# Dividing the last query block's two weight loads into 120 and 8 partitions

## What is computed

```python
q = jnp.einsum('bsd,dq->bsq', h, w_q).reshape(b, s, PEER_HEADS, 2, PEER_HALF)
s1 = jnp.einsum('bshq,hnq->bshn', q[..., 0, :], keys1)
s2 = jnp.einsum('bshq,hnq->bshn', q[..., 1, :], keys2)
v1, i1 = lax.top_k(s1, PEER_TOPK)
v2, i2 = lax.top_k(s2, PEER_TOPK)
...
best, pos = lax.top_k(cand, PEER_TOPK)
expert_idx = jnp.take_along_axis(cand_idx, pos, axis=-1)
gates = jax.nn.softmax(best.astype(jnp.float32), axis=-1).astype(h.dtype)
...
    u = jnp.take(u_tab, ix, axis=0)
    act = jax.nn.gelu(jnp.einsum('chkd,cd->chk', u, hx), approximate=False)
    vv = jnp.take(v_tab, ix, axis=0)
    return jnp.einsum('chk,chkd->cd', gx * act, vv)
```

## Time and profile before

| | us |
|---|---|
| median of 3 runs (1844.26 to 1846.62) | 1845.99 |
| the profiled execution, whole | 1844.33 |
| its span in the trace | 1841.7 |
| DMA from software queue, share of 16 engines | 79.4% |
| DMA from hardware queue, share of 16 engines | 16.5% |
| TensorE busy | 1475.1 |
| VectorE busy | 1142.5 |

### The profile page before, as it was taken

How to read it: one execution, slowest core, us unless ns; L and a number is a source line. 1 busy time by engine, 2 the same in 40 slices (tenths; PEclk the granted TensorE clock), 3 DMA queues, 4 the chain that set the end, 5 groups by cost and what they waited for, 6 DMA issues and landing times.

```text
span 1841.7 us, 13707 instructions
## 1 busy us (share of the span) xinstructions
PE 1475.1 (80%) x4834; PEld 828.1 (45%) x4834; DVE 1142.5 (62%) x1562; ACT 350.9 (19%) x697; POOL 620.3 (34%) x625
## 2 busy tenths in 40 slices
PE   2979998899899897777777777777877777777776
PEld 2549986777788633232323323233322323232332
DVE  5858886688789955555555555538555555544445
ACT  3004332663301211010011101101111111010100
POOL 0001111001154773444343443417643443433341
PEclk9889999999999899999999999998999999999999
DMA  9999998459879999999999999999999999999995
GB/s 341 386 389 404 399 354 326 176 187 379 323 303 413 421 421 421 422 422 422 422 421 422 422 422 422 422 421 402 422 422 422 422 422 421 422 422 422 422 422 233
DMA packets 138241, 716.43 MB, mean 389 GB/s; under 512 B 11158, under 2 KB 15436, under 8 KB 63692
## 3 DMA queue, kind: packets, MB, share of 16 engines
q0 software_dynamic: 82976, 604.02, 79.4%
q1 hardware_dynamic: 55212, 111.77, 16.5%
HBM read 713.65 MB, written 2.10 MB: 389 GB/s over the span
## 4 chain that ended last, share of the span: by engine, by line
DMA 58%; DVE 15%; PE 15%; POOL 6%; issue 4%; ACT 1%; SPq 1%; DVEq 0%; POOLq 0%; ACTq 0%
DMA u_rows<-in_peer_u,expert 49%; DVE u_rows L1740 6%; PE ps L768 4%; DMA v_rows<-in_peer_v,expert 4%; DVE first_acc L454 3%; POOL v_rows L665 3%; POOL u_rows L665 3%; PE ps L762 2%; DMA ada_first<-in_w_ada 2%; PE ps L425 2%; DMA ada_late<-in_w_ada 2%; PE ps L927 2%; DVE ada_acc L293 2%; DMA u_rows<-in_peer_v,expert 1%; PE ps L732 1%
## 5 line engine op out<-in xcount | busy, mean ns | idle before, releaser
L1012 PE MATMUL ps<-v_rows,diag 128*128 128x512 f32 x1960 | 905.6, 608 | 269.8 <-DMA v_rows<-in_peer_v,expert 255.6
L1740 DVE SCALAR_TENSOR_TENSOR u_rows<-u_rows,h 128x2048 f32<-128x2048 f32 x256 | 587.1, 2293 | 519.5 <-DMA u_rows<-in_peer_u,expert 514.7
L1012 PEld LDWEIGHTS ps<-v_rows,diag 128*128 128x128 f32 x1960 | 358.8, 191 | 815.2 <-issue 586.5
L665 POOL DMA_INDIRECT u_rows<-in_peer_u,expert x256 | 284.9, 1113 | 621.1 <-DVE u_rows L1740 576.4
L665 POOL DMA_INDIRECT v_rows<-in_peer_v,expert x249 | 287.2, 1153 | 97.0 <-issue 78.6
L1339 ACT ACTIVATE diag<-ident,hidden 128x128 f32<-128x128 f32 x250 | 89.6, 398 | 847.8 <-PE ps L1012 534.2
L293 DVE SCALAR_TENSOR_TENSOR ada_acc<-ada_late,cact,ada_acc 128x2048 f32<-128x2048 f32 x57 | 133.9, 2349 | 19.5 <-DMA ada_late<-in_w_ada 18.5
L279 POOL DMA_DIRECT2D ada_late<-in_w_ada x61 | 32.4, 532 | 321.9 <-DVE ada_acc L293 275.8
L981 PE MATMUL ps<-h2T,ring 128*128 128x256 f32 x512 | 117.7, 390 | 6.4 <-DMA ring<-in_w_peer_q 6.4
L981 PEld LDWEIGHTS ps<-h2T,ring 128*128 128x128 f32 x512 | 99.6, 197 | 20.6 <-DMA ring<-in_w_peer_q 6.8
L454 DVE SCALAR_TENSOR_TENSOR first_acc<-ada_first,cact,first_acc 128x1024 f32<-128x1024 f32 x60 | 77.0, 1284 | 16.9 <-DMA ada_first<-in_w_ada 11.5
(11 more groups left out here) (273 smaller groups left out, 1256.4 us busy)
## 6 DMA issues: line engine op xcount, KB each, us to landing
ada_late<-in_w_ada POOLq DMA_DIRECT2D x61, 1024.0 KB, 7.7
ada_first<-in_w_ada SPq DMA_DIRECT2D x64, 512.0 KB, 11.7
ring<-in_w_in SPq DMA_DIRECT2D x10, 2048.0 KB, 23.5
ring<-in_w_o SPq DMA_DIRECT2D x8, 2048.0 KB, 19.1
ring<-in_w_peer_q SPq DMA_DIRECT2D x8, 2048.0 KB, 14.3
opened<-in_w_in SPq DMA_DIRECT2D x8, 1024.0 KB, 13.0
u_rows<-in_peer_u,expert POOLq DMA_INDIRECT x256, 32.2
v_rows<-in_peer_v,expert POOLq DMA_INDIRECT x249, 34.2
```

The lines of the kernel that those rows point to most:

```text
L665: nc.gpsimd.indirect_dma_start(buf[:, :], None, table, bass.IndirectOffsetOnAxis(ap=expert[:, q, k:k + 1], axis=0)).then_inc(done, 16)
L1012: ins = nc.tensor.matmul(ps[:, c, :], diag[i % len(diag)][:, :], buf[:, 512 * c:512 * c + 512], start=(n % HALF_SLOTS == 0), stop=last)
L1740: nc.vector.scalar_tensor_tensor(out=buf[:, :], in0=buf[:, :], scalar=1.0, in1=h2[:, q // H, :], op0=ALU.mult, op1=ALU.mult, accum_out=hid ...
```

## The change

Each half of w_pq3 is loaded by two transfers, one of partitions 0 to 119 and one of partitions 120 to 127, issued one behind the other on SP, both on the semaphore of that half of the ring. The plan counts two transfers for each half of that block, so TensorE waits for both. w_pq0 to w_pq2 are loaded as before.

```diff
-    def load_half(eng, name, half, view, col, width=512):
+    def load_half(eng, name, half, view, col, width=512, rows=((0, P),)):
         chunks = slice(KH * half, KH * half + KH)
         w = ring[item[name][0]][:, :].rearrange("p (kc n) -> p kc n", kc=KC)
-        load(eng, name, half, (w[:, chunks, 0:width], view[:, chunks, col:col + width]))
+        load(eng, name, half, *((w[lo:hi, chunks, 0:width], view[lo:hi, chunks, col:col + width]) for lo, hi in rows))
...
     for n in range(4):
-        plan_load(f"w_pq{n}", n % 2, ((q_half_read, n + 1), unit_read(f"p{2 * n + 1}")))
+        plan_load(f"w_pq{n}", n % 2, ((q_half_read, n + 1), unit_read(f"p{2 * n + 1}")), pieces=(2, 2) if n == 3 else (1, 1))
...
             for n in range(2, 4):
                 for half in range(2):
-                    load_half(sp, f"w_pq{n}", half, wpq_view, 512 * n)
+                    load_half(sp, f"w_pq{n}", half, wpq_view, 512 * n, rows=((0, 120), (120, P)) if n == 3 else ((0, P),))
```

## The result

The changed kernel takes 1860.94 us (median of 4 runs, 1856.01 to 1862.79) beside 1845.7 us for the kernel before on the same chip: 15.2 us more, ratio 1.0079, 95% interval 1.0064 to 1.0095. It is slower. The profiled execution took 1862.79 us for a span of 1860.1.

A forecast was written before the change was run, and what follows sets the result against it. DMA bandwidth for the expert gathers was taken as the bound, with one engine 6.1 us late at the end. A gain of 6.0 us, other terms priced zero, gave 1840.0 us against the 1845.99 us median; range 1838.0 to 1847.8 us.

The forecast's parts named there:

- What bounds the kernel: From 640 us on, gathers fill all sixteen DMA engines at 421 to 422 GB/s; one engine ends 6.1 us late.
- The bytes of the block: w_pq3's halves: eight engines get 1.24 us more, seven the same, the one left out 9.9 us less.
- The late engine is the one left out: End of transfers: the cut relieves the engine 6.1 us behind; gain 5.5 to 6.9 us, taken as 6.0; chance 0.58.
- rival B: The late engine is one of eight with nine partitions; its line grows by 1.24 us, 1847.2 us; chance 0.20.
- The 2.0 us to be won back at 1240 us: End of first token tile: idle time of each of fifteen engines waiting for the late one, counted as gain.
- A's own range: The forecast case, engine left out is the late one: 1840.0 us, own range 1838.3 to 1843.0; chance 0.58.
- its smaller gain: Case A if the late engine runs dry once more while GpSimd stands 3.4 us: 2.1 us.
- The load lands later: w_pq3's second half: 6.1 us later, TensorE waits about 12.5 us, GpSimd about 3.4; price zero under queued gathers.
- The cap of the wait's cost: GpSimd's wait for bank p7: zero with 15 us of queued gathers as cover, 3.4 us if that were gone.
- The two added issues: SP's queue: two more transfers at 0.37 us each; price zero, at most 0.74 us on a load.
- Rival C: Nothing moves: late engine keeps eight partitions, or 120 spread over all sixteen and eight fill the gap; 1846.0 us; chance 0.15.
- Rival D: w_pq3 split on too few engines: 10 to 40 us slower; signs: landing over 70 us, below 400 GB/s after 630; chance 0.07.

## Why the prediction was wrong, point by point

**What bounds the kernel: right.** The loss is the bytes not carried between 540 and 690 us, 15.6 us by the windows. Neither TensorE's wait of 24.85 us nor GpSimd's of 8.42 us is on the path beyond 0.7 us.

**The bytes of the block: no run shows which engine got which share, and the shares were not what mattered.** The sum priced a cut by the bytes that it gives to each engine: 1.24 us at most. The step that failed is the one before it, that an engine carries its share at 26.4 GB/s wherever the share lies. The runs with 64 neighbouring and 64 spread partitions (the same count and bytes, 25.6 us apart) show that this is not so, and in the changed kernel the rate fell from 413 to 336 GB/s at the same DMA share. I put all of the 15.2 us to that step, since the windows account for it without another. A lower rate for everything under way had no term, no bound and no rival: the two-sided bound for an operation that the trace doesn't show was taken over bytes and times of landing, and not over the rate.

**The late engine is the one left out: wrong.** The tails with added traffic put it among the first seven of the lowest eight, which is rival B. B's 1847.2 us was off by the same missing term. The reason given for the ends of the row was weak, since nothing in the trace ranked the sixteen, and the chance of 0.58 was far too high for it. Two numbers around it don't follow from the rows either. The 2.0 us to be won back at 1240 us were taken from the rate; the DMA share there, 0.96 instead of 1.02, is worth 15 x 0.06 = 0.9 us. And the upper end of A's own range, 1843.0 us, is not the 1845.99 - 2.1 = 1843.9 of its smaller gain. Neither would have saved the forecast.

**The load lands later: right in kind, off in size.** Expected 6.1 us later and TensorE waiting 12.5 us; it was 23 us and 24.85. The cap of the wait's cost held: GpSimd stood 8.42 us instead of 3.4, and the gathers in the queue covered all but 0.7 us.

**The two added issues: right in that they cost nothing, wrong in their length.** Two transfers by chunks cost nothing (0.9991). But the bound of 0.74 us took each issue at 0.37 us, and the last one of the changed kernel took 24.96:

```profile
560.02 24.96 SPq L247 DMA_DIRECT2D ring<-in_w_peer_q  x1
```

It took 18.0 us in the run with 112 and 16, 8.5 with 64 and 64, 6.0 with even and odd and 5.5 by chunks. The kernel before had shown such issues, though not on this block: its loads of w_in took up to 14.2 us each. SP has nothing else to do there, so the issue itself holds up only the last eight partitions. What it waits for, and whether it makes the second half later, is not shown.

**Rival C** named the rule of the Trainium skill, "DMA: Bandwidth & Descriptors", section "Rules for kernel authors", that two transfers to disjoint partition halves don't pay. The rule speaks of halves, both over all sixteen engines; the prediction took it for any two sets of partitions and read it as "no change". For 64 and 64 neighbouring partitions the measured price is 11 us; for even and odd it is nothing. **Rival D** had the sign and a price of 10 to 40 us, from another mechanism: shares of 16 partitions on eight engines. That the sign agreed is luck. Its own signs did not come (the second half was there 65.7 us after its issue at 559.65, not over 70, and the rate was 415 GB/s from 640 us on), and the runs with 112 and 16 and with 64 and 64, counts with no need for uneven shares, are slow too. The range, which ended at 1847.8 us, left D out by its chance of 0.07.

## What to carry to other kernels

A load cut by neighbouring partitions is not a load with fewer bytes per engine: price its rate, and that of everything under way beside it, before counting bytes, above all where a stage is bound by DMA. If a large load must be in two pieces, cut it along the free dimension and keep all 128 partitions, or take every second partition. One engine that works alone at the end of the transfers stands for some 6 us here by the trace (no run won them back), but find out which one it is, by adding traffic to a few and reading the rate of the tail, before giving it less to do.

## What the hardware showed that was not expected

- Loads of 120, 112 or 64 neighbouring partitions beside gathers lower the rate of all DMA traffic to between 313 and 362 GB/s, where it was between 413 and 421, at an unchanged busy share of 1.02; in the changed kernel the mean packet gets 22% longer on the hardware queue and 25% on the software queue (557 to 579 us).
- With little beside it, a cut load of 120 and 8 partitions ran at 176 GB/s, its packets of 2 KB at 167 ns instead of 94.
- 64 partitions spread over all 128 cost no more than their bytes (420 GB/s), 60 spread ones do (379 GB/s).
- Even small loads slow the rest: 15 partitions of 4 KB at a time, one load under way, held the rate at 383 to 384 GB/s from 1300 to 1425 us, 8 partitions at 389 to 394.
- The issue of one more transfer on SP's queue took 24.96 us in the changed kernel; the eight loads of w_peer_q in the kernel before took 0.37 us each.
- One DMA engine falls 6 us behind the others over 1.2 ms of gathers, and the lag was there again after the cut had disturbed the queues. What makes it late was not tried.
